# Third block's norm by halves, two input blocks projected step by step together, residual behind the first convolutions

## What is computed

```python
# second block, i = 1: latent projections, then the gated embedding
proj = u @ w_in;  cq, ckv, k_rope, z = split(proj)       # 384, 256, 32, 1024 columns
q = rms_norm(cq, q_norm) @ w_qb;  kv = rms_norm(ckv, kv_norm) @ w_kvb
...
gate = sigmoid(rms_norm(h, ple_norm_g[i]) @ ple_w_gate[i])
h = h + (p[i] @ ple_w[i]) * gate
x = rms_norm(h, final_norm_g)                            # the residual of the third block
# third block
h = _rmsnorm(x, norm_w) * (1.0 + scale) + shift
proj = h @ w_in                                          # z, xbc (1280 columns), dt (16), q, k, v, z, f (8), g
xbc = silu(causal_depthwise_conv(xbc, conv_w, conv_b))   # four taps
dt = softplus(dt_raw + dt_bias)
...
```

## Time and profile before

| | us |
|---|---|
| median of 3 runs | 2940.75 |
| lowest, highest | 2934.57, 2943.5 |
| the profiled execution | 2935.45 |
| its span, first to last instruction | 2934.1 |
| TensorE (PE) matmul busy | 2789.7 (95%) |
| TensorE weight load busy | 2277.5 (78%) |
| VectorE busy | 1594.6 (54%) |
| ScalarE busy | 1351.5 (46%) |
| GpSimd busy | 849.5 (29%) |

### The profile page before, as it was taken

The page is one execution under the profiler, slowest core; times in us unless marked ns, Lnnn a source line. Parts: engine busy times, 40 slices in busy tenths (PEclk is TensorE's granted clock), DMA queues, the critical chain, the costliest instruction groups (busy, mean ns, idle before and its releaser), DMA issues.

```text
span 2934.1 us, 36292 instructions
## 1 busy us (share of the span) xinstructions
PE 2789.7 (95%) x13800; PEld 2277.5 (78%) x13800; DVE 1594.6 (54%) x2767; ACT 1351.5 (46%) x2482; POOL 849.5 (29%) x669
## 2 busy tenths in 40 slices
PE   8999999998899999999996999999999999999997
PEld 6878777776788888887774777778787888887875
DVE  6667774633388888887467665532002444433034
ACT  5668854334366666674434334541113333333122
POOL 0334441223344445542121221123221111112331
PEclk9999999999999999999998999999999999999999
DMA  3101141211100000004111110032211001001231
GB/s 130 40 29 41 40 140 54 94 65 36 33 10 10 10 10 10 17 23 144 44 58 73 48 36 22 22 100 84 68 44 43 23 29 36 23 29 48 75 115 72
DMA packets 54443, 148.77 MB, mean 51 GB/s; under 512 B 6144, under 2 KB 14976, under 8 KB 54272
## 3 DMA queue, kind: packets, MB, share of 16 engines
q1 hardware_dynamic: 54272, 146.46, 15.4%
HBM read 129.66 MB, written 16.78 MB: 50 GB/s over the span
## 4 chain that ended last, share of the span: by engine, by line
PE 84%; DVE 7%; ACT 5%; issue 3%; POOL 1%; DMA 0%; ACTq 0%; DVEq 0%; POOLq 0%
PE ps L327 78%; PE ps L417 4%; ACT t L311 1%; PE ps L2515 1%; PE ps L740 1%; DVE t L1604 0%; ACT t L779 0%; DVE t L1894 0%; DVE t L870 0%; DVE t L1786 0%; DVE t L2861 0%; DVE t L839 0%; DVE t L1777 0%; POOL t L318 0%; DVE t L1790 0%
## 5 line engine op out<-in xcount | busy, mean ns | idle before, releaser
L327 PE MATMUL ps<-t,t 128*128 128x512 f32 (+5 forms) x11912 | 2625.6, 379 | 113.2 <-issue 12.8
L327 PEld LDWEIGHTS ps<-t,t 128*128 128x128 f32 (+2 forms) x11912 | 2075.5, 185 | 592.8 <-issue 113.5
L318 POOL TENSOR_TENSOR t<-t,t 128x1024 fp32r<-128x1024 f32 (+2 forms) x169 | 355.1, 2102 | 1286.9 <-ACT t L311 1286.4
L311 ACT ACTIVATE t<-t 128x1024 fp32r<-128x1024 f32 (+2 forms) x205 | 187.0, 912 | 651.5 <-PE ps L327 651.4
L1660 POOL TENSOR_SCALAR t<-t,t 128x1024 f32<-128x1024 f32 x128 | 145.5, 1137 | 182.9 <-DVE t L1610 179.9
L1604 DVE TENSOR_TENSOR t<-ps,t 128x512 fp32r<-128x512 f32 x256 | 164.3, 682 | 15.7 <-ACT t L1521 13.9
L417 PE MATMUL ps<-t,t 128*128 128x128 f32 x1176 | 160.5, 274 | 12.8 <-DVE t L1604 7.6
L417 PEld LDWEIGHTS ps<-t,t 128*128 128x128 f32 x1176 | 131.8, 141 | 36.8 <-issue 25.0
L1617 DVE TENSOR_REDUCE t<-ps 128x1 f32<-128x1024 f32 x128 | 154.1, 1204 | 1.8 <-PE ps L327 1.8
L1521 ACT ACTIVATE t<-ps 128x512 fp32r<-128x512 f32 x256 | 140.2, 591 | 11.3 <-PE ps L417 7.2
L1529 ACT ACTIVATE t<-ps,t 128x1024 f32<-128x1024 f32 x128 | 142.9, 1117 | 1.9 <-DVE t L1617 1.5
(11 more groups left out here) (223 smaller groups left out, 2426.6 us busy)
## 6 DMA issues: line engine op xcount, KB each, us to landing
t<-in_wflat SPq DMA_DIRECT2D x156, 512.0 KB, 3.6
t<-in_wada SPq DMA_DIRECT2D x48, 256.0 KB, 4.3
t<-in_xT SPq DMA_DIRECT2D x16, 512.0 KB, 6.9
t<-in_wflat SPq DMA_DIRECT2D x32, 128.0 KB, 2.0
hd<-t SPq DMA_DIRECT2D x8, 512.0 KB, 3.0
t<-hd SPq DMA_DIRECT2D x8, 512.0 KB, 7.2
x2d<-t SPq DMA_DIRECT2D x8, 512.0 KB, 2.6
md<-t SPq DMA_DIRECT2D x16, 256.0 KB, 4.3
```

Source lines behind the costliest of these rows:

```text
L311: ac.activation(parts(i)[0][:, 0:n], raw[i % 2][:, 0:n], ACT.Copy).then_inc(*on.up(ac, "whi", i))
L318: e.tensor_tensor(lo[:, 0:n], raw[i % 2][:, 0:n], hi[:, 0:n], ALU.subtract) \
L327: return pe.matmul(o, l, r, start=start, stop=stop)
```

## The change

Five things are changed.

1. The last row (7, second half) of the second embedding: DVE adds it to h itself, in place of POOL. The squares of row (7, first half) go ahead of its gate on ACT and DVE, and DVE joins RB and RC of the first half before the sum over the partitions (`both_squares`), so that one sum is enough for C. The high part of the second xbc block goes behind its Sigmoid. Its own squares are made inside the norm stage.
2. The norm by halves: `total_c(0)` and Ln, Exp of the first half (`root(0)`), then rows of the first half; `root(1)` stands on ACT behind the high part of row 4. `total_c(1)` and the two sums for D run on PE within the projection.
3. `lin_pair`: blocks 0 and 1 of xbc are projected together, six matmuls at each k, first half in banks 0 and 1, second half in banks 2 and 3. The sum for C stands ahead of k = 3 of the first half, the sums for D ahead of k = 5 of the second.
4. The convolutions: root of D on ACT straight after the norm; the order of the first half blocks is 0, 1 (first half), 0, 1 (second half). ACT makes the high parts of dt and block 2 after the copy of the second half block, and takes Silu one half block later than it did. The 16 operations of the residual stand on DVE behind the taps of blocks 0 and 1; its stores stand on SP behind the load of a later block. Half block 2, first half, is projected ahead of the transposes of dt.
5. Stage B: the first latents in the order q 0, q 1 (first half), q 0, q 1 (second half); the high part of Z1 is made between the two halves of the q norm, that of Z2 ahead of the k norm; their low parts are moved likewise on POOL.

The core of the diff:

```diff
+        def lin_pair(ij, hf, banks, hi, lo, need, frees, at_k, mid):
+
+            for i, b in zip(ij, banks):
+                on.wait_ge(pe, "whi", i)
+                on.wait_ge(pe, low(i), i)
+                wait_bank(b)
+                bank[i, hf] = b
+            for k in range(8):
+                if k == at_k:
+                    mid()
+                for event in need(k, hf):
+                    on.wait_ge(pe, *event)
+                for i, b, ends in zip(ij, banks, frees):
+                    nk, m, wh, wl = block(i)
+                    t = mm3(ps[0:m, b, :], wh[:, k, :], wl[:, k, :], hi[:, k, half(hf)], lo[:, k, half(hf)], k == 0, k == 7)
+                    if k == 7:
+                        t.then_inc(*on.up(pe, "mm", i, hf))
+                        freed[b] = list(ends)
...
+        def halves(n, first=False, last=False):
+
+            todo = [(x, hf) for x in range(n) for hf in range(2)]
+            if first:
+                todo[1], todo[2] = todo[2], todo[1]
...
-                        users.append((("sq2", *rows_done[m - 1]), ("acc", "C", *rows_done[m - 1])))
+                        of_row.append((("sq2", *rows_done[m - 1]), ("acc", "C", *rows_done[m - 1])))
+                users += of_row[1:] + of_row[:1] if j and m == len(rows_done) - 1 else of_row
...
+                        if is_last(n, hf):
+                            read_on_vector(*prev)
+                            both_squares(0)
...
-                        if prev:
+                        if is_last(n, hf):
+                            h = hT[:, n, half(hf)]
+                            on.wait_ge(dv, "gated", j, n, hf)
+                            on.wait_ge(dv, "uh", st, n, hf)
+                            dv.tensor_tensor(h, h, t, ALU.add).then_inc(*on.up(dv, "gated/h2", j, n, hf))
+                        elif prev:
                             read_on_vector(*prev)
-                read_on_vector(*rows_done[-1])
+                if j == 0:
+                    read_on_vector(*rows_done[-1])
...
+            def both_squares(hf):
+
+                rc = RC[:, half(hf)]
+                on.wait_ge(dv, "acc", "D", 7, hf)
+                on.wait_ge(dv, "acc", "C", 7, hf)
+                dv.scalar_tensor_tensor(rc, RB[:, half(hf)], EPS, rc, ALU.mult, ALU.add).then_inc(*on.up(dv, "norm/both", hf))
...
-                    if hf:
+                    if hf and not (done and is_last(n, hf)):
                         w_hi(i + 2)
                     if done:
                         if (n, hf) in firsts:
                             rstd(st, hf, tbank[hf], RA, T)
+                        if is_last(n, hf):
+                            read_on_scalar(*prev)
                         t = T_["gate", n, hf][0]
                         on.wait_ge(ac, "gate scaled", j, n, hf)
                         ac.activation(t, t, ACT.Sigmoid).then_inc(*on.up(ac, "gate", j, n, hf))
-                        if prev:
+                        if is_last(n, hf):
+                            w_hi(i + 2)
+                        elif prev:
                             read_on_scalar(*prev)
-                read_on_scalar(*rows_done[-1])
+                if j == 0:
+                    read_on_scalar(*rows_done[-1])
...
-                    if done:
+                    if done and not is_last(n, hf):
...
+            first = [(*lat[x], hf) for x, hf in halves(5, first=True)]
+            T_sq = tmps([((w, k, hf), ("acc", w, k, hf)) for w, k, _, hf in first if k])
...
+                for w, k, i, hf in first:
+                    bank[i, hf] = lin(i, hf, next_bank(*every), Uh, Ul, need_u, [("latent", w, k, hf)])
+                    if (w, k) == ("q", 0):
+                        bank["B", hf] = next_bank(*every)
+                        total("B", hf, bank["B", hf], RB, ("acc", "B", 7, hf))
...
-            def normed_hi(w, C, T_):
+            def normed_hi(w, C, T_, between):
                 name = "c" + w
                 for hf in range(2):
+                    if hf == (w == "q"):
+                        w_hi(between)
...
-                normed_hi("q", CQ, T_q)
-                w_hi(LR + 2)
-                normed_hi("k", CK, T_k)
...
+                normed_hi("q", CQ, T_q, LR + 2)
+                normed_hi("k", CK, T_k, Z[0] + 2)
                 for n, i in zip(Z_ORDER, Z):
                     for hf in range(2):
-                        if hf:
+                        if hf and i != Z[0]:
                             w_hi(i + 2)
...
+                    if hf:
+                        w_lo(po, LR + 2)
...
-                        w_lo(po, LR + 2)
+                        w_lo(po, Z[0] + 2)
...
-                for i in Z:
+                for i in Z[1:]:
...
-            for hf in range(2):
-                for st, acc in (("D", RB), ("C", RC)):
-                    b = bank[st, hf] = next_bank(*every)
-                    total(st, hf, b, acc, ("acc", st, 7, hf))
-                    freed[b] = [("norm/both", hf)]
+            both_squares, read_on_vector, read_on_scalar = last_row
+            total_c(0)
...
-                    on.wait_ge(dv, "norm/first", hf)
-                    dv.tensor_tensor(rc, ps[:, bank["C", hf], :], rb, ALU.add).then_inc(*on.up(dv, "norm/both", hf))
...
+
+                normed(0, 0)
+                normed(1, 0)
+                low_part(0, 0)
+                read_on_vector(7, 1)
+                both_squares(1)
+                for k in range(2, 8):
+                    normed(k, 0)
+                    low_part(k - 1, 0)
+                low_part(7, 0)
+                normed(0, 1)
+                for k in range(1, 8):
+                    normed(k, 1)
+                    low_part(k - 1, 1)
+                low_part(7, 1)
...
+                root(0)
...
+                high_part(0, 0)
+                read_on_scalar(7, 1)
+                for k in range(1, 5):
+                    high_part(k, 0)
+                root(1)
+                for k in range(5, 8):
+                    high_part(k, 0)
                 for k in range(8):
-                    on.wait_ge(sp, "x2 out", k, 1)
-                    sp.dma_start(x2d[k], hT[:, k, :]).then_inc(*on.landed(sp, "x2d", k))
-
-            vector()
-            scalar()
-            sync()
-
-        stage_norm()
+                    high_part(k, 1)
+
+            def root(hf):
+                rc = RC[:, half(hf)]
+                on.wait_ge(ac, "sums/tot", "C", hf)
+                ac.activation(rc, ps[:, bank["C", hf], :], ACT.Ln, bias=eps[:, 1:2], scale=1.0 / T).then_inc(*on.up(ac, "ln", "C", hf))
+                on.wait_ge(ac, "ln", "C", hf)
+                ac.activation(rc, rc, ACT.Exp, scale=-0.5).then_inc(*on.up(ac, "rstd", "C", hf))
...
+        def total_c(hf):
+            b = bank["C", hf] = (4, 5)[hf]
+            total("C", hf, b, RC, ("norm/both", hf))
+
+        def totals_d():
+            for hf in range(2):
+                b = bank["D", hf] = 6 + hf
+                total("D", hf, b, RB, ("acc", "D", 7, hf))
+
+        norm_vector, norm_scalar = stage_norm()
...
-                for q, n in enumerate(X_ORDER):
-                    if n == 2:
+
+                lin_pair(XB[0:2], 0, (0, 1), Uh, Ul, need_c, [[("conv in", q, 0)] for q in range(2)], 3, lambda: total_c(1))
+                lin_pair(XB[0:2], 1, (2, 3), Uh, Ul, need_c, [[("conv in", q, 1)] for q in range(2)], 5, totals_d)
+                for q, n, hf in todo[4:]:
+                    if (n, hf) == (2, 0):
+                        for x in range(2):
+                            bank[DTF, x] = lin(DTF, x, next_bank(*every), Uh, Ul, need_c, [("dt", x)])
+                    if (n, hf) == (2, 1):
                         step_sizes()
-                    if n == 4:
+                    if (n, hf) == (4, 0):
                         cumsums()
-                    for hf in range(2):
-                        bank[XB[q], hf] = lin(XB[q], hf, next_bank(*every), Uh, Ul, need_c, [("conv in", q, hf)])
+                    bank[XB[q], hf] = lin(XB[q], hf, next_bank(*every), Uh, Ul, need_c, [("conv in", q, hf)])
...
+                norm_vector()
                 for i in range(2):
                     z = dv.memset(xin[i][:, 0:3], 0.0)
+                z.then_inc(*on.up(dv, "steps/xin zero"))
+                for q, n, hf in todo:
+                    if (n, hf) == (2, 0):
+                        residual()
+                        softplus()
+                    if (n, hf) == (4, 0):
+                        sums()
...
+            def residual():
+                for k in range(8):
+                    for x in range(2):
+                        h = hT[:, k, half(x)]
+                        on.wait_ge(dv, "rstd", "D", x)
+                        dv.scalar_tensor_tensor(h, h, v("fng", k), RB[:, half(x)], ALU.mult, ALU.mult).then_inc(*on.up(dv, "x2 out", k, x))
                 on.wait_ge(dv, "x2 out", 7, 1)
                 dv.memset(SG[:, :].bitcast(F32), 0.0)
```

(26 more changed lines are left out.)

194 lines of the change are left out of this document (78 added, 116 removed).

## The result

The changed kernel takes 2922.57 us in the median of its first runs (2921.96 to 2923.54), beside 2940.61 for the kernel before (2934.57 to 2943.5): 18.0 us less, ratio 0.9942, 95% interval 0.9924 to 0.9959. A second set of runs gave 2921.06 against 2940.33, ratio 0.9939 (0.9925 to 0.9954; brackets behind a ratio are its interval from here on). The forecast was 2923.0.

What follows compares the result with a forecast made beforehand. PE was taken to bound the kernel (84% of the chain), so only its waits and low clock could be won. 11.1 + 6.6 = 17.7 us off the median 2940.75 gave 2923.0, range 2913 to 2932.

Steps and rivals of the forecast that it cites:

- First root: Last row of the second embedding and root of the first half: first norm operation, at 1563.80 before, 7.0 us earlier.
- Pair until its end: Blocks 0 and 1 projected together: end at 1589.0 against 1597.87, 39.7 us after the last gate matmul (before 48.6).
- bank rotation decides: dt's first half falls in bank 2, whose copy on ACT stands behind Silu and taps, so dt starts at 1599.3.
- Start of dt: dt starts at 1599.3 against 1605.85, 6.5 us earlier, after PE has stood 10.3 us.
- Behind dt: Block 2's first half covers the 3.55 us except transposes (some 0.8); its second half starts 11.1 us earlier; nothing stalls behind.
- Stage B: Waits of 5.37 and 3.67 us ahead of Z1 and Z2 go, 4.1 ahead of Z3 comes: 6.6 us won.
- Sum: Whole change: 11.1 us up to block 2's second half plus 6.6 in stage B, 17.7 us.
- Span and median: Profiled execution 2935.45 less 17.7 gives 2917.7; it lies 5.3 under the median of the runs, so 2923.0 was predicted.
- The rival on table loads: By the skill Ln then Exp need one load: three roots each 1.3 us shorter, gain some 4 us larger; no chance given.
- Rival D: Low clock stays through the paced pair: block 2's first half ends 13 us later, less 6.6 from stage B; chance 0.03.
- The bound of loss in D: From 17.7 us of work at the low clock beyond the sum the change is a loss; one more block makes 2956.
- for those of 7 us and more: PE's clock: the trace agrees with the skill's throttling rule for gaps of 7 us and more, disagrees for short gaps.

## Why the prediction was right, point by point

- **First root** (7.0 us earlier): gate to first norm operation 7.4 us against 7.5 foretold. Right; the join of the squares ended 1.2 us behind the last gate matmul, 1.3 foretold.
- **Pair until its end** (39.7 us behind the last gate matmul): 39.6. Right in its steps: row 1 late by 0.43, a rest of 1.41 at row 5 behind the root of the second half, then no rest for 70 matmuls. The clock rose 4 to 5 us after the start, 5.9 taken (stretches of 4 us, third column from the end):

```profile
1555.00:1559.00 4.00, 3.38 (x7) 2.32 (x8) 3.89 (x8) 1.72 (x3) 0.00 (x0) 0.50 0.00 0
1559.00:1563.00 4.00, 4.00 (x15) 2.83 (x14) 4.00 (x7) 2.73 (x3) 0.00 (x0) 0.88 0.01 2
```

  Small errors lie inside: row 0 took 2.90 us, not 2.57. What the prediction leaves unsaid is that the pair is worth next to nothing here. It prints the pair's end in bold as if it were a gain, while its own next step ("bank rotation decides") has dt wait 10.3 us behind that end. The run without the pair shows that the end can lie 6 us later at a loss of 1.7 us in place: ACT's queue, DVE's taps and bank 2 set dt, and the pair lay beside them. The sum was not harmed, since dt's start was worked out from ACT.
- **Start of dt** (6.5 us earlier): 7.4 measured; rest 10.3 foretold, 9.51 measured. The parts: roots of D 7.8 against 7.87 (1579.61 to 1587.48), POOL's share in the taps 2.4 against 4.50 - 2.33 = 2.17, shown by the run that moved it; bank 2 as the last wait, shown by the run with other banks. The sum goes from row to row and nowhere says what the residual's new place is worth; the run with the residual in front shows that 12.1 of the 12.5 us hang on it.
- **Behind dt**: no wait but the transposes of 0.67, as foretold. Whole stretch 80.4 to 67.9, 12.5 us, where the sum had 11.1; 0.9 of the difference lies ahead of dt, 0.5 behind it.
- **Stage B**: rests ahead of Z1 and Z2 gone, 4.42 ahead of Z3 against 4.1. I had given half of 2.75 to the clock, which makes 7.6 - 1.4 = 6.2 and not the 6.6 that I wrote, a slip. The clock fell, and Z3 and what follows took 2.1 us longer by it: 5.2 in place. By medians the part alone gave 6.5.
- **Sum**: 12.5 + 5.2 = 17.7 in place, 17.7 foretold (17.3 without the slip). The two errors, +1.4 and -1.4, cancel by chance.
- **Span and median**: the step that missed is the one that set the sum against the profiled execution, 2917.7; the profiled execution of after took 2922.75, its span 2921.4 where 2934.1 - 17.7 = 2916.4. I took the untouched 1300 us behind as fixed, and they are not: behind the same wait of 3.54 us the same matmuls took 2.45 us longer in after. The medians differ by 18.0 and 19.3 us, close to the 17.7; that is luck in part, since with other banks, with two loads and with the later high part of block 2 the median moved by 2.3 to 4.4 us more than the place. The difference between profile and median of before, 5.3 us, was a warning of this that I only carried along.
- **The rival on table loads**: each Exp is preceded by a load of 1.28 us behind Ln in after as well (1563.81 above), and with Ln, Ln, Exp, Exp for D, two loads fewer, dt came 2.8 us forward. The Trainium skill ("ScalarE: Activation LUTs", "Table sets: the hidden batching unit") says that Ln and Exp share one load; these traces disagree for this program. It also advises to batch by set; the run with two loads agrees.
- **Rival D** (clock stays low) fell. In after the rests of 7.44 and 9.51 us are followed by 0.50, as are those of 6.68 and 7.98 us before; inside the pair, with rests of 0.43 and 1.41, the clock rose and stayed up. The run that kept PE busy shows that the low start of the pair cost 0.6 us. The Trainium skill has the rule weighed with it ("TensorE: Matmul & The Clock Gate", "HAM oscillation — how this bites in real kernels"), that bursts parted by waits start low each time; the traces agree for the long rests. But the line that I drew, "for those of 7 us and more", is too high: before, the clock is 0.50 behind the rests of 5.37 and 4.28 us too, and without the pair behind one of 2.74; it is 1.00 behind 3.67 in one place and behind 3.54 in another.
- **The bound of loss in D** is misworked: I let 17.7 us of work at the low clock undo the gain. That much delay takes 17.7 / (1 - 0.233 / 0.428) = 39 us of work at the low clock.

## What to carry to other kernels

Follow a wait back to the queue that ends it before pricing what stands in front of it: here a bank of the ring, freed by a copy behind a Silu behind taps behind table loads, decided, and the largest rearrangement on PE brought 1.7 us in place and nothing in the time while that stood (and 2.5 us in place once it was mended), and the place of 16 side operations on DVE brought 12.1. Look at what bank the ring deals out after hand-picked banks; a choice of two free banks gave 8.4 us, 4.0 of them in place. And take differences within one trace, from event to event, for the mechanism, and medians for the time: the two profiled spans of the changed kernel differ by 1.9 us, the profiled execution of before and its median by 5.2.

## What the runs showed of the hardware

- The same wait costs different times in different traces: with the same 3.54 us rest the clock behind it was 1.00 in one trace and 0.50 in another, worth 2.45 us over 543 matmuls. Local gains of 4.0 and 1.6 us became 8.4 and 3.9 in the median, in the first case only partly by the clock. Why a rest of given length lets the clock fall in one run and not in another was not settled here.
- dt and the first half of block 2 start slow after rests of 20.4, 9.5, 7.5, 6.7, 5.0, 3.7 and 2.2 us alike (72 matmuls in 19.5, 18.3, 19.1, 19.6, 18.8, 19.6 and 18.4 us): starting them earlier by 2.0 and 2.8 us gave back 0.9 and 1.3 of it.
- A first tap beside POOL takes 2.60 us in place of 0.54, three further taps 4.50 in place of 2.33; moving POOL's operation by one half block moves the cost with it.
